# Stick-breaking attention in a streaming encoder step: the prompt's heads taken in pairs, as half-array matmuls

## What is computed

```python
z = einsum('bqhd,bkhd->bhqk', q_blk, keys) * SB_SCALE      # 8 heads, d = 64
visible = arange(keys) < q_idx
log_keep = where(visible, log_sigmoid(-z), 0)
tail = cumsum(log_keep, axis=3, reverse=True) - log_keep
weight = where(visible, exp(log_sigmoid(z) + tail), 0)
out = einsum('bhqk,bkhd->bqhd', weight, vals)
```

## Time and profile before

| | before |
|---|---|
| median of 3 runs | 874.61 us |
| the profiled execution | 873.39 us |
| its span, first to last instruction | 871.5 us |
| mean granted TensorE clock | 0.986 |
| PE busy | 839.4 us, 96% |
| DVE, ACT, POOL busy | 416.1, 364.9, 120.6 us |

### The profile page before, as it was taken

The page is one execution under the profiler, slowest core; times in us unless marked ns, Lnnn a source line. Parts: engine busy times, 40 slices in busy tenths (PEclk is TensorE's granted clock), DMA queues, the critical chain, the costliest instruction groups (busy, mean ns, idle before and its releaser), DMA issues.

```text
span 871.5 us, 15008 instructions
## 1 busy us (share of the span) xinstructions
PE 839.4 (96%) x5970; PEld 806.8 (93%) x5971; DVE 416.1 (48%) x667; ACT 364.9 (42%) x609; POOL 120.6 (14%) x132
## 2 busy tenths in 40 slices
PE   3999999999999999999999999999999999999994
PEld 2899899989988887999999999999999999999994
DVE  6734334564444445886765454323225454432444
ACT  4433425545544445555454444222224444322323
POOL 5430000560000000005550000000000000012431
PEclk9899999999999998999999999999999999999998
DMA  9422241111111110225111223232223223222202
GB/s 356 169 93 86 73 129 50 49 52 49 49 49 50 49 49 25 74 82 185 49 50 43 80 80 89 73 97 72 83 85 81 89 72 96 72 89 82 73 12 99
DMA packets 21919, 71.49 MB, mean 82 GB/s; under 512 B 2336, under 2 KB 6576, under 8 KB 21488
## 3 DMA queue, kind: packets, MB, share of 16 engines
q1 hardware_dynamic: 21040, 67.97, 24.4%
q0 software_dynamic: 544, 2.52, 0.9%
q10 hardware_dynamic: 288, 0.33, 0.1%
HBM read 65.96 MB, written 4.85 MB: 81 GB/s over the span
## 4 chain that ended last, share of the span: by engine, by line
PE 92%; DVE 4%; ACT 2%; DMA 1%; SPq 1%; issue 0%; ACTq 0%; DVEq 0%
PE lin L446 17%; PE lin L447 17%; PE lin L448 17%; PE lin L910 4%; PE lin L909 4%; PE lin L908 4%; PE z L660 3%; PE lin L780 3%; PE lin L781 3%; PE lin L782 3%; PE xo L711 2%; PE z L646 2%; PE xo L448 1%; PE xo L447 1%; PE xo L446 1%; PE z L635 1%
## 5 line engine op out<-in xcount | busy, mean ns | idle before, releaser
L446 PE MATMUL lin<-h_hi,whi 128*128 128x288 f32 (+1 forms) x832 | 247.1, 297 | 0.0
L447 PE MATMUL lin<-h_lo,whi 128*128 128x288 f32 (+1 forms) x832 | 245.9, 296 | 0.0
L448 PE MATMUL lin<-h_hi,wlo 128*128 128x288 f32 (+1 forms) x832 | 245.0, 294 | 0.0
L448 PEld LDWEIGHTS lin<-h_hi,wlo 128*128 128x128 f32 x832 | 156.6, 188 | 0.0
L447 PEld LDWEIGHTS lin<-h_lo,whi 128*128 128x128 f32 x832 | 156.4, 188 | 0.1
L446 PEld LDWEIGHTS lin<-h_hi,whi 128*128 128x128 f32 x832 | 156.4, 188 | 0.1
L949 ACT ACTIVATE whi<-raw 128x1024 fp32r<-128x1024 f32 x92 | 96.8, 1052 | 139.9 <-PE lin L448 65.7
L1480 DVE TENSOR_TENSOR wlo<-raw,whi 128x1024 fp32r<-128x1024 f32 x82 | 101.3, 1236 | 72.3 <-ACT whi L949 69.6
L448 PE MATMUL lin<-f_hi,wlo 128*128 128x288 f32 x256 | 75.5, 295 | 0.0
L447 PE MATMUL lin<-f_lo,whi 128*128 128x288 f32 x256 | 75.4, 294 | 0.0
L446 PE MATMUL lin<-f_hi,whi 128*128 128x288 f32 x256 | 75.3, 294 | 0.0
(11 more groups left out here) (308 smaller groups left out, 1728.7 us busy)
## 6 DMA issues: line engine op xcount, KB each, us to landing
raw<-w_stream SPq DMA_DIRECT2D x112, 512.0 KB, 3.6
r<-x_t SPq DMA_DIRECT2D x8, 296.0 KB, 5.9
y<-r SPq DMA_DIRECT2D x16, 144.0 KB, 1.9
kcache<-k_cache SPq DMA_DIRECT2D x1, 2048.0 KB, 13.9
vcache<-v_cache SPq DMA_DIRECT2D x1, 2048.0 KB, 10.5
k_new<-k_t POOLq DMA_DIRECT2D x1, 1184.0 KB, 4.8
v_new<-v_t POOLq DMA_DIRECT2D x1, 1024.0 KB, 5.8
wpool<-w_pool ACTq DMA_DIRECT2D x1, 256.0 KB, 3.6
```

Source lines behind the costliest of these rows:

```text
L446: pe.matmul(out, w_h, hi, start=first, stop=False)
L447: pe.matmul(out, w_h, lo, start=False, stop=False)
L448: return pe.matmul(out, w_l, hi, start=False, stop=last)
```

## The change

The eight items of the prompt become four pairs of items. The first item of a pair, late, has the key blocks 2, 3 and 4 of both heads (432 columns for each head, 864 in all); the second, early, has the blocks 1 and 0 (912 for each, 1824 in all). `is_late(i)` tells them apart.

- Scores: `q_t` holds two heads on the halves of the partitions as `k_t` does, and each matmul uses 64 partitions of both: head 0 of the pair on partitions 0 to 63, head 1 on 64 to 127, alternating, into different PSUM banks. The running stream's queries are in a tile of their own, `q_s`, with the zeros (POOL clears 512 columns in place of 4608).
- Weighted values: the stationary is 64 columns, one head's; head 0 goes to partitions 0 to 63 of one bank `pair_out`, head 1 to 64 to 127, alternating. A pair is taken out by one 128x512 instruction on ACT and one on DVE after the early item.
- ACT and DVE take both heads in one instruction with a two-part access (`128x2x400` for 800 columns).
- The early item's sum over the late blocks comes from the late item's `sp_hi` and `sp_lo`, which are kept.
- `suffix_sums` signals twice an item, so that the early item's Exp of block 1 starts before block 0's sums are in.
- The halves: `SHARES` gives item 0 none, items 1 and 2 3 and 1 as before, late items 2 and 1, early items 4 and 1, the last one too.

```diff
-OFF = [sum(QW[:b]) for b in range(5)]
+LATE_AT, LATE_W = {2: 0, 3: QW[2], 4: QW[2] + QW[3]}, QW[2] + QW[3] + QW[4]
+EARLY_AT, EARLY_W = {0: 0, 1: BANK}, BANK + QW[1]
...
-BEFORE = [[]] + [HALVES[4 * i - 2:4 * i + 1] for i in range(1, ITEMS - 1)] + [HALVES[-2:]]
-AFTER = [HALVES[:2]] + [HALVES[4 * i + 1:4 * i + 2] for i in range(1, ITEMS - 1)] + [[]]
+SHARES = [(0, 0), (3, 1), (3, 1)] + [(2, 1), (4, 1)] * 4
...
-        q_t = sb("q_t", [HEADS, TA], F32, A0 + 11584)
+        q_t = sb("q_t", [PAIRS, SEQ], F32, A0 + 11584)
+        q_s = sb("q_s", [HEADS, DEC], F32, A0 + 13632)
...
-        z = ctx.enter_context(nc.psum_tensor("z", [P, 3, BANK], F32))
-        xo = ctx.enter_context(nc.psum_tensor("xo", [P, 2, BANK], F32))
+        z = ctx.enter_context(nc.psum_tensor("z", [P, 5, BANK], F32))
+        xo = z[:, 3:5, :]
+        pair_out = z[:, 4, :]
...
-                h = i - 3
-                for b in range(5):
+                pair, blocks = (i - 3) // 2, (2, 3, 4) if is_late(i) else (1, 0)
+                for n, b in enumerate(blocks):
                     k0 = min(b * P, TAIL)
-                    for dst, at, w in bank_pieces(OFF[b], QW[b]):
-                        pe.matmul(zf[:, dst:dst + w], k_t[:, h // 2, k0:k0 + P],
-                                  q_t[:, h, QS[b] + at:QS[b] + at + w],
-                                  start=(dst % BANK == 0), stop=True, skip_group_check=True)
+                    for e in range(2):
+                        rows, at = slice(64 * e, 64 * e + 64), z_of(e, b)
+                        pe.matmul(zf[:, at:at + QW[b]], k_t[rows, pair, k0:k0 + P], q_t[rows, pair, QS[b]:SEQ],
+                                  start=at % BANK == 0, stop=True, skip_group_check=True)
...
+                    for n, b in enumerate((2, 3, 4) if late else (1, 0)):
+                        if n == 1:
                             pe.wait_ge(w_done, 2 * i + 2)
...
+                        for e in range(2):
+                            rows, src = slice(64 * e, 64 * e + 64), e * w + (LATE_AT if late else EARLY_AT)[b]
+                            vals = v_t[:, b, pair * P + 64 * e:pair * P + 64 * e + 64]
+                            last = pe.matmul(pair_out[rows, QS[b]:SEQ], vals, sa[:, src:src + QW[b]],
+                                             start=b == 2, stop=b == 0, skip_group_check=True)
...
+                    absolute(i, 0)
+                    absolute(i, 1)
+                    exponential(i, 0)
+                    after_half(*BEFORE[i][0])
+                    exponential(i, 1)
+                    logarithm(i, 0)
+                    logarithm(i, 1)
+                    after_half(*BEFORE[i][1])
+                    sums_hi(i)
```

More of the change, by code:

```diff
@@ L57, with is_late @@
 ITEMS = 3 + HEADS
+ZS = 3 * BANK
+LATE_AT, LATE_W = {2: 0, 3: QW[2], 4: QW[2] + QW[3]}, QW[2] + QW[3] + QW[4]
+EARLY_AT, EARLY_W = {0: 0, 1: BANK}, BANK + QW[1]
+SP_LATE = 2 * EARLY_W
+SP_W = SP_LATE + 2 * LATE_W
+def is_late(i):
+    return i >= 3 and (i - 3) % 2 == 0
 def pieces(i):
-    return [(p * BANK, (p + 1) * BANK) for p in range(3)] if i < 3 else [(OFF[2], ZP), (0, OFF[2])]
+    if i < 3:
+        return [(p * BANK, (p + 1) * BANK) for p in range(3)]
+    return [(LATE_AT[3], LATE_W), (0, LATE_AT[3])] if is_late(i) else [(BANK, EARLY_W), (0, BANK)]
 def split_at(i, p):
-    return (3 * i + p) % SLOTS * BANK if i < 3 else pieces(i)[p][0]
+    return (3 * i + p) % SLOTS * BANK
 def pieces_before(i):
@@ L672, in suffix_sums @@
                     return
[L673 to L688, removed]
+                late, w = is_late(i), LATE_W if is_late(i) else EARLY_W
+                for p in range(2):
+                    pe.wait_ge(splo_done, pieces_before(i) + p + 1)
+                    for b in ((4, 3), (2,))[p] if late else ((1,), (0,))[p]:
+                        for e in range(2):
+                            dst = z_of(e, b)
+                            if b < 4:
+                                last = subtract(dst, tri_r, sp_of(e, b), QW[b])
+                            if b < 3:
+                                last = subtract(dst + QS[b + 1] - QS[b], below_r, sp_of(e, b + 1), QW[b + 1])
+                            if b >= 3:
+                                const = tri if b == 4 else below
+                                at, src = dst + QS[4] - QS[b], e * w + LATE_AT[4]
+                                last = pe.matmul(zf[:, at:at + QW[4]], const[:, :], sa[:, src:src + QW[4]],
+                                                 start=False, stop=True, skip_group_check=True)
+                    last.then_inc(tri_done, 1)
             def weighted_values(i):
@@ L1115, in _ @@
                 act.wait_ge(half_done, N_Q + m + 1)
[L1116 to L1120, removed]
+                nc.scalar.activation(q_t[:, m, 0:HA], lin[:, 0, 0:HA], ACT.Identity, bias=bq8[:, m:m + 1],
+                                     scale=SB_SCALE).then_inc(bank_free[0], 1)
             act.wait_ge(made, 7)
@@ L1124, in _, with absolute, exponential, logarithm @@
             nc.scalar.activation(below_r[:, :], below[:, :], ACT.Copy).then_inc(consts, 1)
-            def softplus_tail(i):
[L1128 to L1137, removed]
+            def absolute(i, p):
+                a, b = pieces(i)[p]
+                if p == 0:
+                    act.wait_ge(qk_done, i + 1)
+                src, out = (zf[:, a:b], sa[:, a:b]) if i < 3 else (both_z(i, a, b), both(sa, i, a, b))
+                nc.scalar.activation(out, src, ACT.Abs).then_inc(abs_done, 1)
+            def exponential(i, p):
+                a, b = pieces(i)[p]
+                at = sa[:, a:b] if i < 3 else both(sa, i, a, b)
+                act.wait_ge(abs_done, pieces_before(i) + p + 1)
+                nc.scalar.activation(at, at, ACT.Exp, scale=-1.0).then_inc(expn_done, 1)
+            def logarithm(i, p):
+                a, b = pieces(i)[p]
+                at = sa[:, a:b] if i < 3 else both(sa, i, a, b)
+                act.wait_ge(expn_done, pieces_before(i) + p + 1)
+                nc.scalar.activation(at, at, ACT.Ln, bias=1.0).then_inc(ln_done, 1)
+            def softplus_tail(i):
+                n = len(pieces(i))
+                for p in range(n):
+                    absolute(i, p)
+                for p in range(n):
+                    exponential(i, p)
+                for p in range(n):
+                    logarithm(i, p)
             def pool_output_hi():
@@ L1174, in head_out_hi @@
                 else:
[L1175 to L1178, removed]
+                    nc.scalar.activation(attn_hi[:, (i - 3) // 2, 0:SEQ], pair_out, ACT.Copy).then_inc(attn_hi_done, 1)
             def after_half(u, h):
@@ L1688, in softplus, with add @@
                 n = pieces_before(i)
-                def add(cols, term, first):
+                def add(out, term, first):
                     nonlocal run
@@ L1777, in _ @@
             for i in range(ITEMS):
+                early = i >= 3 and not is_late(i)
+                if early:
+                    after_half(*BEFORE[i][0])
                 softplus(i)
@@ L1781, in _ @@
                 sums_lo(i)
-                for u, h in BEFORE[i]:
+                for u, h in BEFORE[i][1 if early else 0:]:
                     after_half(u, h)
```

151 lines of the change are left out of this document (96 added, 55 removed).

## The result

| | before | after |
|---|---|---|
| median | 874.01 us (4 runs) | 851.09 us (4 runs, 850.62 to 851.53) |
| the profiled execution's span | 871.5 us | 848.8 us |
| mean granted TensorE clock | 0.986 | 0.990 |

The ratio is 0.9746, 95% interval 0.9729 to 0.9762: 2.5% faster, 22.9 us where 13.6 were forecast. The kernel before spreads more from run to run (870.4 to 875.1) than the changed one.

A forecast was written before the change was run, and what follows sets the result against it. PE, busy 96% of the span, was taken as the bound. 13.6 + 1.9 + 0.35 + 5.45 - 0.95 - 6.75 = 13.6 us off 873.39 gave 859.8, median 861.0; own range 854 to 864, with A 854 to 870 (about 80%).

The forecast's parts named there:

- Scores and values: Prompt attention on PE: two heads side by side on array halves, 3.4 us saved a pair, 13.6 us over four pairs.
- Changes of shape: PE switching between whole array, column halves and row halves: 25 changes at 0.27 us, 6.75 us lost, ends 0 and 8.75.
- Item 3: Item beside POOL with one half fewer: second low part near 7.6, wanted at 7.4; counted 0, ends 2 lost and 1 gained.
- Suffix sums and masks: PE's own work: two fp32r matmuls fewer a head, 1.9 us, and fewer masks, 0.35 us; between 1.5 and 2.5.
- The last item: Item 10: four halves before the suffix sums fill PE's waits and avoid the half clock; 5.45 us gained, ends 3 and 5.5.
- Item 0: Its halves go elsewhere, so its weighted values wait for the last bias add: 0.95 us lost, 3 more if the clock fell.
- The chains: ACT and DVE work stays hidden behind PE's halves: 1.0 and 0.9 us to spare in early items, 0.2 in item 10.
- the slower rival: Early item's ACT and DVE chain outgrows its four halves, PE waits and clock halves: 21.8 us, 882.8; chance 7%.
- A: Rival: only one kind, say row halves but not column halves, runs side by side; price 6.6 us, 867.6; chance 13%.
- B: Rival: neither scores nor weighted values run side by side, shape switches still paid; 874.6, with ends 867.9 to 876.6; chance 10%.
- The lag: Scores and weighted values: second head's stream starts one pass after the first, 0.32 us early, 0.24 late, by PE's program order.

## Why the prediction was wrong

The direction, the cause and most terms held; the size didn't. The step that failed is the one on scores and weighted values, with the price of the changes of shape behind it.

- **Scores and values.** "The second starts one pass after the first, since every matmul is two passes on its own half and PE starts them in order." PE doesn't: both heads' passes start together (178.27 x2), and head by head the order in the program costs nothing until head 1's first pass stands six behind. A pair was put at 6.32 us without the changes of shape. By the steps in the middle of the streams (0.34, 0.43, 0.23, 0.12 and, for two passes of 16 columns, 0.14) two heads take 1.53 early and 0.84 late for each kind, 4.74 for a pair. That is 1.58 us a pair, 6.3 us of the miss.
- **Changes of shape.** Put at 0.27 each (25, 6.75 us), between 0 and 0.35. A pair's scores and values take 5.38 us where the bare streams take 4.74, and its halves 0.2 more than before: 0.8 for six changes, 0.13 each. The count was short as well: behind items 6 to 9 PE does matmuls of the pooling branch between the values and the scores, so there is one change more, and each of these places grew by 0.2 us (0.7 in all). The changes come to 3.9 us, so 2.8 of the miss. Tail and load were added up as if the one had to end before the other began; the rows bounded the price but don't show why it is less. Not all of it is the change's own: the first pass of the scores was 0.08 longer than its like before too (0.51 for 0.43 at 190.94), with no change of shape.
- **Item 3** was counted at 0, between 2 lost and 1 gained. Its two waits and what stood about them are gone: 1.3 gained. The reason given was that it waited before too. But the chain worked out for it would end about when PE wants it, and so it did: DVE's second low part ended at 172.87, 7.4 us after the first Abs (7.6 expected), and PE took it at 173.03 without a wait. That wait, gone, should have stood in the sum.
- **Suffix sums and masks** were put at 2.25 us. A pair has 0.44 + 0.04 less: 1.9.
- **The last item** was put at 5.45. Alone, on the kernel before, it gave 5.5, less the wait at item 0. In the changed kernel the clock stays at 1.00 there, and item 10 is 0.3 longer than item 4: 5.2.
- **Item 0**: 0.95 expected; the wait is 0.94 and there is no fall of the clock (1.00 in 110 to 125). From the start of its sums to the end of its values, the halves left out, item 0 is 1.2 longer.
- **The chains** came where the working put them. In item 10 DVE's last low part ended 13.9 us after the first Abs (13.8 expected), at 309.95; PE started on it at 310.01 and had stood for 0.14 us, too little for the view of waits. In the other early items the view lists no wait, so the slower rival fell; A and B fell with the passes that start together.

The lag and the changes are 9.1 us together against a miss of 9.2 (859.8 forecast for the profiled execution, 850.6 measured); item 3 adds 1.3, and the smaller terms take that back.

The range failed for one reason: its lower end took the changes of shape at nothing, but kept the lag as if it were certain. Both ends of that had to be carried too: with no lag the prediction's own costs make 4 x 1.21 = 4.84 of a pair's 6.32, and the same sum gives 861.0 - 5.9 = 855.1, and 848.3 with the changes at nothing. Its upper end was added up wrong, without effect here: 861.0 + 2.0 + 2.7 is 865.7, not 864. The chance of faster (0.87) is also more than its parts, which make 0.84.

In the profile's terms: 17.4 (scores and values with the changes in them) - 0.7 (the step ahead of the values) - 0.7 (the changes about the pooling matmuls) + 1.9 + 1.3 (item 3) + 5.2 - 1.2 (item 0) = 23.2, where the two spans differ by 22.7. Of the 0.5 that is left, 0.2 is that item 0's sums start later (115.25 for 115.08); the rest isn't assigned.

## What to carry to other kernels

Where a matmul uses half of the rows or half of the stationary columns, put the other half's next to it: here 38.9 us of passes became about 23, changes of shape included. Alternate the halves, as only a few passes ahead are reached, and group each kind, as every change costs 0.1 to 0.2 us. And when the work beside a chain of waits shrinks, look first at the item that has too little filler: its waits cost their length, and then the half clock behind them (0.50 in 335 to 337 before, 0.56 in 315 to 320 with the halves as before).

## What the runs showed of the hardware

- Two halves of the array start passes together even where one stands four passes behind the other in the program (179.72, twice, with all four of one head ahead of the other's first); six ahead, the second half starts with the first half's third pass (202.87 and 180.09), so four behind was reached and five wasn't. That the reach is counted in passes rather than in something else was not tried.
- fp32 passes of 400 and 512 columns lose nothing to each other as column halves, each with its own 128 partitions of moving data (1.68 in place of 3.20), nor as row halves into two banks (steps of 0.34 and 0.43, as for one pass before).
- A change of shape costs 0.11 (row halves to whole array) to 0.20 us (whole array to row halves), 0.13 on average in the changed kernel and 0.155 in the run with more of them; part of it lies in the step of the last matmul ahead of the change. The Trainium skill (TensorEngine Tiling (Array Packing), Key Properties) says that a change drains TensorE; by that rule the trace agrees in kind, with 0.155 us for one in the late items.
